# Three-term split products for the key queries, the cross-attention queries and four output products, with the extra weight slots placed behind the cross-attention

## The reference, cut to what matters

```python
qry = (h @ w_q).reshape(B, S, PEER_HEADS, PEER_DKEY)      # key queries: 256x1024 @ 1024x2048
...
# second block, once per layer (two layers), alpha = 4 ** 0.25
x = layer_norm(alpha * x + mixed @ w_out, g, b)           # w_out: ab_w_out (layer 0), mla_w_out (layer 1)
q = x @ wq                                                # cross-attention queries: 1024x1024
x = layer_norm(alpha * x + attended @ wo, g, b)           # wo: 1024x1024
x = layer_norm(alpha * x + moe(x), g, b)                  # 32 experts, top 2, router first
```

## Time and profile before

| | |
|---|---|
| median of 3 runs | 2772.55 us (2771.01 to 2774.83) |
| the profiled execution, its own time | 2769.58 us |
| its span, first to last instruction | 2767.9 us |
| PE busy | 2532.1 us, 91% of the span |
| DVE, ACT busy | 1094.6 us (40%), 663.3 us (24%) |
| HBM traffic | 650.28 MB, mean 235 GB/s; 426 GB/s in the expert stages |
| granted PE clock, mean | 0.97 of full |

### The profile page before, as it was taken

How to read it: one execution, slowest core, us unless ns; L and a number is a source line. 1 busy time by engine, 2 the same in 40 slices (tenths; PEclk the granted TensorE clock), 3 DMA queues, 4 the chain that set the end, 5 groups by cost and what they waited for, 6 DMA issues and landing times. The chain is left out here.

```text
span 2767.9 us, 41173 instructions
## 1 busy us (share of the span) xinstructions
PE 2532.1 (91%) x16034; PEld 1795.6 (65%) x16034; DVE 1094.6 (40%) x2311; ACT 663.3 (24%) x1240; POOL 124.4 (4%) x180
## 2 busy tenths in 40 slices
PE   8989987899999999999989799998888979998987
PEld 6648656799999999977856455444455645554443
DVE  1241979666666666644442311111134232111112
ACT  2120129544444444433211100000013111000000
POOL 1020000000000000000200000000002000000000
PEclk9999999999999999999989799999989989999999
DMA  5315420355555555555134399999961635999996
GB/s 203 112 64 194 152 81 0 122 188 183 187 192 182 186 189 186 184 192 208 62 141 170 135 427 426 426 426 427 426 229 66 243 129 245 426 426 426 426 428 282
DMA packets 130166, 650.28 MB, mean 235 GB/s; under 512 B 14179, under 2 KB 25190, under 8 KB 95590
## 3 DMA queue, kind: packets, MB, share of 16 engines
q1 hardware_dynamic: 118080, 628.19, 57.7%
q10 hardware_dynamic: 11958, 20.25, 2.2%
HBM read 642.12 MB, written 6.29 MB: 234 GB/s over the span
## 5 line engine op out<-in xcount | busy, mean ns | idle before, releaser
L474 PE MATMUL banks<-peer_input_high,u_high 128*128 128x256 f32 x1024 | 290.6, 284 | 4.4 <-DVE u_low L1549 4.4
L3080 DVE COPY expert_hidden_T<-banks 128x256 f32<-128x256 f32 x64 | 27.2, 425 | 667.5 <-PE banks L2834 667.5
L474 PE MATMUL banks<-peer_input_high,u_low 128*128 128x256 f32 x1024 | 290.8, 284 | 0.0
L474 PE MATMUL banks<-peer_input_low,u_high 128*128 128x256 f32 x1024 | 290.8, 284 | 0.0
L474 PE MATMUL banks<-weight_ring,window_rows_T 128*64 128x256 f32 x1984 | 224.7, 381 | 30.4 <-DMA weight_ring<-in_moe_w_up 27.4
L474 PEld LDWEIGHTS banks<-weight_ring,window_rows_T 128*64 128x64 f32 x1984 | 145.7, 137 | 115.4 <-DMA weight_ring<-in_moe_w_up 37.4
L474 PEld LDWEIGHTS banks<-peer_input_high,u_high 128*128 128x128 f32 x1024 | 197.2, 193 | 9.9 <-DVE u_low L1549 5.1
L1517 PE MATMUL banks<-v_high,gated_high 128*128 128x512 f32 x512 | 200.9, 392 | 0.0
L1517 PE MATMUL banks<-v_low,gated_high 128*128 128x512 f32 x512 | 200.7, 392 | 0.0
L1541 ACT ACTIVATE v_high<-v_of_key 128x1024 fp32r<-128x1024 f32 x128 | 135.7, 1060 | 270.0 <-PE banks L1517 270.0
L474 PEld LDWEIGHTS banks<-peer_input_low,u_high 128*128 128x128 f32 x1024 | 197.2, 193 | 4.8
(11 more groups left out here) (451 smaller groups left out, 3615.8 us busy)
## 6 DMA issues: line engine op xcount, KB each, us to landing
weight_ring<-in_moe_w_down SPq DMA_DIRECT2D x44, 2048.0 KB, 38.3
weight_ring<-in_moe_w_up SPq DMA_DIRECT2D x40, 2048.0 KB, 38.1
v_of_key<-in_peer_v_rows SPq DMA_DIRECT2D x128, 512.0 KB, 3.3
x<-in_peer_u_T SPq DMA_DIRECT2D x128, 512.0 KB, 4.4
more_weight_slots<-in_moe_w_up SPq DMA_DIRECT2D x24, 2048.0 KB, 35.1
weight_ring<-in_moe_w_gate SPq DMA_DIRECT2D x22, 2048.0 KB, 32.7
more_weight_slots<-in_moe_w_gate SPq DMA_DIRECT2D x22, 2048.0 KB, 36.9
gain_bias_h_T<-in_moe_w_gate SPq DMA_DIRECT2D x20, 2048.0 KB, 37.6
```

What stands on the lines that cost most here:

```text
L474: return k.nc.tensor.matmul(out, lhsT, rhs, start=start, stop=stop)
L3080: nc.vector.tensor_copy(b.hid_T[:, e % 2, :, :].rearrange("p m n -> p (m n)"), k.ps[:, TURN_BANK, 0:2 * P]).then_inc(k.turned_copied.up(), 1)
```

## The change

It adds a class that splits both factors piece by piece, ACT making `high` and DVE `low` beside PE, and uses it for the key queries and both cross-attention queries (`split_features`) and for the four output products (`norm_and_turn`). A piece is two of the eight rows of chunks: 128 x 1024 of the weights, 128 x 512 of the inputs. It also moves `more_slots` from before the cross-attention to after it. Cut to its core:

```diff
+class HighLow:
+    PIECES = 4
...
+    def input_high(self, act, i):
+        self.k.nc.scalar.activation(self.x_high[:, 2 * i:2 * i + 2, :], self.x[:, 2 * i:2 * i + 2, :],
+                                    ACT.Copy).then_inc(self.k.inputs_high.up(), 1)
...
+    def weight_high(self, act, n):
+        if n % self.PIECES == 0:
+            self.k.stream.wait_landed(act, self.tiles[n // self.PIECES])
+        if n >= self.PIECES:
+            act.wait_ge(self.k.products.sem, self.k.products.at(n - self.PIECES + 1))
+        self.k.nc.scalar.activation(self.high(n), self.raw(n), ACT.Copy).then_inc(self.k.weights_high.up(), 1)
+    def weight_low(self, dve, n):
+        dve.wait_ge(self.k.weights_high.sem, self.k.weights_high.at(n + 1))
+        self.k.nc.vector.tensor_tensor(self.low(n), self.raw(n), self.high(n),
+                                       ALU.subtract).then_inc(self.k.weights_low.up(), 1)
+    def terms(self, pe, n, product):
+        ch0 = 2 * (n % self.PIECES)
+        pe.wait_ge(self.k.weights_high.sem, self.k.weights_high.at(n + 1))
+        if n < self.PIECES:
+            pe.wait_ge(self.k.inputs_high.sem, self.k.inputs_high.at(n + 1))
+        for c in range(2):
+            product(self.high(n)[:, c, :], self.x_high[:, ch0 + c, :], ch0 + c == 0, False)
...
+            product(self.high(n)[:, c, :], self.x_low[:, ch0 + c, :], False, False)
+        pe.wait_ge(self.k.weights_low.sem, self.k.weights_low.at(n + 1))
+        for c in range(2):
+            last = product(self.low(n)[:, c, :], self.x_high[:, ch0 + c, :], False, ch0 + c == DC - 1)
...
+def split_features(k, first, tiles, x, out, scale=None, loads=()):
...
+                k.stream.prefetch(sp, first + tiles, first, {first + i: pieces * (i + 1) for i in range(tiles)},
+                                  pieces * tiles)
...
+                for dst, src in loads:
+                    act.dma_start(dst, src).then_inc(k.small_loaded.up(16), 16)
+                for n in range(pieces * tiles):
+                    if n < pieces:
+                        parts.input_high(act, n)
+                    parts.weight_high(act, n)
+                    if n % pieces == 2 and n > pieces:
+                        copied(n // pieces - 1)
+                copied(tiles - 1)
...
 def norm_and_turn(k, x, gb, loads, products=None, hT=None, out=None, eps=1e-5):
...
-                    k.stream.prefetch(sp, first + 2, first, {first: 3, first + 1: 4})
+                    k.stream.prefetch(sp, first + 2, first, {first: 4, first + 1: 6})
...
-                    for tt, j in ((0, 0), (0, 1), (1, 0)):
-                        projected(tt, j)
+                    for n in range(4):
+                        projected(n, (0, 1)).then_inc(k.products.up(), 1)
+                    for tt in range(NT):
+                        for n in range(4, 8):
+                            last = projected(n, (tt,))
+                        last.then_inc(k.products.up(), 1)
                 if hT is not None:
-                    turned(0)
-                if products:
-                    projected(1, 1)
-                if hT is not None:
-                    turned(1)
+                    for tt in range(NT):
+                        turned(tt)
...
                 for dst, src in loads:
                     act.dma_start(dst, src).then_inc(k.small_loaded.up(16), 16)
+                if products:
+                    for n in range(8):
+                        if n < 4:
+                            parts.input_high(act, n)
+                        parts.weight_high(act, n)
...
+                if products:
+                    for n in range(8):
+                        if n < 4:
+                            parts.input_low(dve, n)
+                        if n == 7:
+                            summed(0, 0)
+                        parts.weight_low(dve, n)
+                    summed(1, 0)
...
@@ second_block
+            cross_attention(k, x, hT, layer, tiles, gb, norm_loads(2, layer) + router_loads(layer))
             more = c.enter_context(ExitStack())
             more_ring = sb("more_weight_slots", [P, MORE_SLOTS, SLOT], ctx=more)
             k.stream.more_slots(more_ring)
-            cross_attention(k, x, hT, layer, tiles, gb, norm_loads(2, layer) + router_loads(layer))
             moe(k, x, layer, tiles, router, hT, gb, norm_loads(3, layer), ninth, more_ring[:, 0, :],
```

More of the change, by code:

```diff
@@ L269, in __init__ @@
         self.x_in_banks = signal("x_in_banks")
+        self.inputs_high = signal("inputs_high")
+        self.inputs_low = signal("inputs_low")
+        self.weights_high = signal("weights_high")
+        self.weights_low = signal("weights_low")
         self.scores_ready = signal("scores_ready")
@@ L521, in norm_and_turn @@
         half_of = lambda tt, j: x[:, tt, j * 512:(j + 1) * 512]
+        if products:
+            xT, first = products
+            parts = HighLow(k, [first, first + 1], xT, c)
+            done = {(0, 0): 4, (1, 0): 4, (0, 1): 5, (1, 1): 6}
         with k.stage() as block:
@@ L537, in _, with projected, product @@
             def _(pe):
[L538 to L546, removed]
+                def projected(n, tokens):
+                    j = n // parts.PIECES
+                    def product(w, x_part, start, stop):
+                        for tt in tokens:
+                            last = nc.tensor.matmul(k.ps[:, 2 * tt + j, :], x_part[:, tt * P:(tt + 1) * P], w,
+                                                    start=start, stop=stop)
+                        return last
+                    return parts.terms(pe, n, product)
                 def turned(tt):
@@ L591, in _, with summed @@
                 v = nc.vector
-                for tt in range(NT):
[L593 to L600, removed]
+                def summed(tt, j):
+                    if products:
+                        dve.wait_ge(k.products.sem, k.products.at(done[tt, j]))
+                        k.v(v.scalar_tensor_tensor(out=half_of(tt, j), in0=half_of(tt, j), scalar=ALPHA,
+                                                   in1=k.ps[:, 2 * tt + j, :], op0=ALU.mult, op1=ALU.add))
+                    v.bn_stats(st[:, tt, j, :], half_of(tt, j) if products else k.ps[:, 2 * tt + j, :]
+                               ).then_inc(k.half_summed.up(), 1)
+                if products:
+                    for n in range(8):
+                        if n < 4:
+                            parts.input_low(dve, n)
+                        if n == 7:
+                            summed(0, 0)
+                        parts.weight_low(dve, n)
+                    summed(1, 0)
+                for tt in range(NT):
+                    for j in range(1 if products else 0, 2):
+                        summed(tt, j)
+                    dve.wait_ge(k.half_summed.sem, k.half_summed.at(3 + tt if products else 2 * (tt + 1)))
                     k.v(v.bn_aggr(mv[:, tt, :], st[:, tt, :, :].rearrange("p a b -> p (a b)")))
@@ L1260, in peer_routing @@
         memT = sb("memory_2_T", [P, DC, S], ctx=c)
[L1261 to L1263 removed]
+        split_features(k, tiles["w_peer_q"], 4, hT, lambda m: qT[:, m, :], None,
+                       [(hT_keep, hT[:, :, :])] + [(sub[:, n, :, :], k.dram[f"subkeys_T_{n + 1}"]) for n in range(2)]
+                       + [(iota[:, :], k.const("iota")[:, 0:TOPK]), (memT[:, :, :], k.dram["mem_2_T"])])
         sc = sb("sub_scores", [P, 2, NT, PH, PK], ctx=c)
@@ L2568, in cross_attention @@
         v = sb("xa_v", [P, NT, D], ctx=c)
[L2569 to L2575, removed]
+        split_features(k, t0, 2, hT, lambda m: q_T[:, m, :], XA_D ** -0.5,
+                       [(k_T[:, :, :], k.dram["xa_k_T"][layer]), (v[:, :, :], k.dram["xa_v"][layer])])
         outT = q_T
```

69 lines of the change are left out of this document (63 added, 6 removed).

## The result

| | before | changed |
|---|---|---|
| median of 4 runs each, us | 2772.35 | 2790.93 (2789.77 to 2792.52) |
| ratio of the two | | 1.0065, interval 1.005 to 1.0079 |
| profiled execution, its span, us | 2769.6, 2767.9 | 2791.77, 2790.1 |
| PE busy, us | 2532.1 | 2499.5 |

The account below looks back on a forecast made before the run. PE's products set the length of the touched stages; router and expert stages are the exceptions, the latter DMA-bound. Split stages -3.0 and router stages +20.2 make +17.2 on the median 2772.55: 2790 us, range 2777 to 2797.

Parts of the forecast that it names:

- The moved slots: Router stage: ACT's small loads take turns with three tiles packet by packet, 17.4 us against 7.3, +10.1 a layer, +20.2.
- upper bound: Router stages: if ACT's last packets came with all 7.4 MB, 17.3 + 1.8 = 19.1 us, +23.6 in two layers.
- against each goes one of SP's of 16 KB, of which there are 384 ... a third of the key rows is through by then: Router stage: each ACT row waits for one 16 KB tile packet; the 86 key rows left cost 1.4 MB, 3.3 us.
- 1.1 + 3.3 + 0.7: Router stage: issue at 1.1 us, 3.3 for the remaining key rows, 0.7 to the signal.
- 128 x 20 KB: Router stage: each 4 KB row of gain or bias goes with a 16 KB tile packet; 256 such cost 12.3 us.
- What comes ahead of the first product: Head of split stages: PE waits for ACT's small-load issues, then 1.9 us for the high parts and signal.
- What a product costs: Split matmuls on PE take 120 ns at 256 columns, 229 at 512; 41 us won if nothing else came with it.
- The rival by the gap that the Trainium skill gives: Split products: PE streams faster, 109 and 216 ns a matmul, giving 2777 us; chance 0.03.
- The cold start: Split stages after PE's wait: half clock over some 4.2 us loses 1.85 us at 256 columns, 1.95 at 512.
- counted at half with 1.0: MLA's output product: 3.4 us of idle is near the edge of a cold start, so 1.0 us was counted.
- The cover: Split stages: ACT and DVE make the parts beside PE, costing nothing as long as they keep up.
- The sum: Whole kernel: -3.0 from the split stages and +20.2 from the router stages, +17.2 us, 2790 us.

Follow-up runs that it names:

- the shorter rows: Changed kernel with each of the three tiles loaded in the router stage issued as four loads of 512 KB with 4 KB rows; 2778.1 us.
- the nine loads behind the parts: Changed kernel, with ACT issuing the nine small loads of the cross-attention's output product behind the first three or more high parts; 2777.66 us.
- the run with filled starts: Kernel with later slots and small loads behind first parts, plus six unread identity products at the head of each split stage; 2743.49 us.
- the slots out of the way: Changed kernel with the three extra slots opened behind the router stage, their tiles issued with the ninth; 2768.27 us, ratio 0.9987.
- both remedies: Changed kernel with slots opened behind the router stage and, in all seven split stages, small loads issued behind the first parts; 2746.63 us.

## Why the prediction was right, point by point

- **The moved slots**, the term that decides: +20.2 forecast for two layers. Measured, the router stages grew by 11.6 and 11.7 us (19.0 and 19.1 against 7.4), +23.3, near the upper bound of 23.6. That the length of the other queue's rows counts is shown by the shorter rows. By the Trainium skill (DMA: Bandwidth & Descriptors, "Queues, rings and completion order") the queues take turns packet by packet. A packet there is a group of descriptors, while the packets of the profile are here single rows of a tile, and the landings agree with turns in direction only: up to the landing of the bias SP's queue had moved 527 packets and 6.03 MB and ACT's 432, not one for one. Together that is 7.1 of the 7.4 MB, so this run alone would as well fit the upper bound, where ACT's last packets come with all the bytes; the shorter rows tell the two apart, since there the bias came after 3.65 MB. The size was off by 1.5 us a layer, in the step "against each goes one of SP's of 16 KB, of which there are 384 ... a third of the key rows is through by then". The keys landed with the whole gate tile, at 8.5 us, 3.4 us more than 1.1 + 3.3 + 0.7: the stage moved 90 and 147 GB/s in its first two us where I had given it one at most, and by the landing SP's queue had moved 2.81 MB where the step has 1.4. The gain came 6.2 us later (1528.20 + 14.3 against 1527.82 + 8.5), as 128 x 20 KB had it. The down tile's rows, though, are 8 KB, and there are 256 of them: the bias took 3.9 us behind the gain (1528.69 + 17.7), close to the 3.7 us of 128 x 12 KB and not 6.2. The two errors partly cancel; 0.4 us more lie between that landing and the end of the stage.
- **What comes ahead of the first product**: 1.9 us from the last issue; measured 1494.53 to 1496.20, 1.7. Key queries, first and cross-attention output products were forecast at 55.3, 33.8 and 40.2, and came at 55.1, 33.7 and 40.4 to 40.9. The run with the nine loads behind the parts shows that it is the issuing that PE waits for.
- **What a product costs**: at the full clock 227 ns a matmul of 512 columns and 120 of 256 (eight start in 0.96 us, 1437.94 to 1438.90 in the timeline of the run with filled starts). The rival by the gap that the Trainium skill gives (TensorE: Matmul & The Clock Gate, "Back-to-back issue gap"), which wanted 109 and 216, is out.
- **The cold start**, 1.85 and 1.95 us a stage from 4.2 us at half clock, was too small. In the queries the products went slowly for 5.2 us (1439.03 to 1444.25); in the cross-attention output 16 matmuls took 6.54 us (1496.20 to 1502.74) where they need 3.63, 2.9 us more. The queries lost 2.3 and MLA's product, counted at half with 1.0, 1.7. A tail and a wait a few tenths shorter than counted hid this in the stages' lengths, but not in MLA's, which came 1.1 us over its 32.8: its parts were ready 0.6 us later than counted, too. That the term is real shows the cross-attention's output product with the loads behind the first parts: after the same 2.55 us of idle it took 33.8 us with a cold start and 32.7 at the full clock. Which starts are cold was not foreseen and is not explained.
- **The cover**: no idle time of PE between pieces; the parts cost nothing beside it, as forecast.
- **Not foreseen**: the attention stage of layer 0 was 21.8 us and not 23.5, though the change does not touch it. The two attention windows of the kernel before, layer 0 and layer 1, and layer 0's of the run with only the slots moved:

```profile
1471.70:1495.20 23.50, 20.09 (x96) 17.22 (x96) 5.98 (x16) 7.65 (x21) 4.74 (x8) 0.93 0.25 90
2204.90:2227.00 22.10, 18.42 (x96) 15.87 (x96) 5.98 (x16) 7.71 (x22) 4.74 (x8) 1.00 0.26 96
...
1474.75:1496.55 21.80, 18.42 (x96) 15.87 (x96) 5.98 (x16) 7.65 (x21) 4.75 (x8) 1.00 0.26 97
```

The same 96 matmuls took 20.09 and 18.42 us, at a clock of 0.93 and of 1.00. The 1.7 us are a clock that fell once in the profiled execution before. They are not won by the splits: the run with only the slots moved, with the old products, has 21.8 us as well. How often the clock falls there in the kernel before one trace of it does not show.
- **The sum**: -3.0 + 20.2 forecast. By the windows it was -0.3 in the seven split stages, -2.1 in the two attentions, +23.3 in the router stages: +20.9 of the 22.2 us between the spans, which is 5.0 more than the 17.2 forecast. The profiled execution before was 2.8 us under its median and the one after 0.8 over its own, so the medians differ by 18.6. So the split stages won 2.7 us less than forecast and the router stages cost 3.1 more, and of this the attention's 2.1 and the 3.6 us between the profiled executions and their medians hid most. The mechanism, its direction and its main term were right; that 2790 met 2790.9 so closely was luck.

## What to carry to other kernels

A small load is priced by its rows, not its bytes, as soon as another queue moves long rows: 20 KB in 128 rows beside 16 KB rows cost 2.8 us here. Before moving bulk loads, look for what short loads the new stage waits for at its end. And where an engine gets new work ahead of the first product, look at what it issues before that: here 7 us of DMA issues took back what the faster product won, and moving them behind the first parts was worth more (21.6 us) than the split products had won with the slots out of the way (3.4).

## What the runs showed of the hardware

- Issuing a load holds ACT for 0.34 to 0.60 us, but the one of the group bias for 3.21, the fifth of nine in a row (3.31 in the kernel before); the expert bias behind it, loaded in the same way, took 0.46. It is not the load itself: issued with a part made between the loads, the same one took 0.35 us in both layers of two runs (the nine loads behind the first parts, and both remedies). What it waits for behind the four others, two of them loads of the router's weights, was not tried.
- After 2.55 us of idle the next products ran at half clock in both layers of one run and at full clock in both layers of another, with the same instructions on PE in the stage.
- Cutting rows from 16 and 8 KB to 4 KB made the last small load of the other queue land 7 us earlier. Up to that landing SP's queue moved 1.6 packets for each of ACT's, and 1.2 with the long rows, not one.
